# Second half of both value stages: nine couples of weight pieces as 2x2 block products, seven products for eight

## What is computed

```python
def peer_ffn(h, wq, keys, u, v):
    ...
    gates = jax.nn.softmax(sc, axis=-1)
    ...
        act = jax.nn.gelu(jnp.einsum('td,ted->te', ht, u[et]), approximate=False)
        return jnp.einsum('te,ted->td', gt * act, v[et])
```

## Time and profile before

| | |
|---|---|
| runs | 2201.31 us median (2198.94, 2201.31, 2205.94) |
| span of the profiled execution | 2200.3 us |
| PE busy | 2187.5 us, 99% |
| DVE busy | 1649.6 us, 75% |
| ACT busy | 1223.3 us, 56% |
| granted PE clock | full in all slices |

### The profile page before, as it was taken

How to read it: one execution, slowest core, us unless ns; L and a number is a source line. 1 busy time by engine, 2 the same in 40 slices (tenths; PEclk the granted TensorE clock), 3 DMA queues, 4 the chain that set the end, 5 groups by cost and what they waited for, 6 DMA issues and landing times.

```text
span 2200.3 us, 43642 instructions
## 1 busy us (share of the span) xinstructions
PE 2187.5 (99%) x14230; PEld 1905.3 (87%) x14230; DVE 1649.6 (75%) x3276; ACT 1223.3 (56%) x1933; POOL 719.4 (33%) x737
## 2 busy tenths in 40 slices
PE   9999999999999999999999999999999999999999
PEld 8899888888888888888988888888888888899887
DVE  8776885888888755666678678888886556558895
ACT  6555555555544445565565555554444446566764
POOL 1506886333344100002088853324440001530000
PEclk9999999999999999999999999999999999999999
DMA  5265665555655566554556655555556665545665
GB/s 175 97 200 156 189 188 176 172 172 170 187 177 179 180 193 191 172 192 134 173 172 186 188 180 173 172 167 187 174 179 193 203 194 172 163 141 159 187 190 162
DMA packets 109819, 385.88 MB, mean 175 GB/s; under 512 B 12545, under 2 KB 15009, under 8 KB 109473
## 3 DMA queue, kind: packets, MB, share of 16 engines
q1 hardware_dynamic: 106864, 382.34, 55.8%
q10 hardware_dynamic: 2864, 2.36, 0.3%
HBM read 383.46 MB, written 1.06 MB: 175 GB/s over the span
## 4 chain that ended last, share of the span: by engine, by line
PE 92%; DVE 5%; POOL 1%; DMA 1%; ACT 1%; issue 1%; SPq 0%; ACTq 0%; DVEq 0%; POOLq 0%
PE bank L2395 24%; PE bank L2367 13%; PE bank L2447 11%; PE bank L2449 11%; PE bank L2448 11%; PE bank L2283 3%; PE bank L2271 3%; PE bank L2275 3%; PE bank L2807 3%; PE bank L2590 1%; DVE w_lo L1259 1%; POOL big L506 1%; PE bank L2491 1%; PE bank L2492 1%; PE bank L2493 1%; PE bank L2775 1%
## 5 line engine op out<-in xcount | busy, mean ns | idle before, releaser
L583 ACT ACTIVATE w_hi<-ring 128x1024 fp32r<-128x1024 f32 x699 | 738.1, 1057 | 509.5 <-PE bank L2449 362.9
L1259 DVE TENSOR_TENSOR w_lo<-ring,w_hi 128x1024 fp32r<-128x1024 f32 x548 | 670.3, 1225 | 261.7 <-ACT w_hi L583 261.7
L2395 PE MATMUL bank<-x_parts,w_hi 128*128 128x512 f32 x2320 | 583.1, 393 | 0.3 <-ACT w_hi L583 0.3
L2395 PEld LDWEIGHTS bank<-x_parts,w_hi 128*128 128x128 f32 x2320 | 416.9, 189 | 75.0 <-issue 0.4
L467 POOL TENSOR_TENSOR w_lo<-ring,w_hi 128x1024 fp32r<-128x1024 f32 x151 | 364.2, 2418 | 266.0 <-DVE x_parts L1244 160.4
L2447 PE MATMUL bank<-w_hi,x_parts 128*128 128x512 f32 x1024 | 400.8, 391 | 0.0
L2449 PE MATMUL bank<-w_lo,x_parts 128*128 128x512 f32 x1024 | 398.7, 389 | 0.0
L2448 PE MATMUL bank<-w_hi,x_parts 128*128 128x512 f32 x1024 | 398.3, 389 | 0.0
L479 POOL COPY quads<-sco 128x32 f16 (+1 forms) x256 | 226.2, 912 | 445.7 <-DVE sco L1751 445.6
L2367 PEld LDWEIGHTS bank<-x_parts,w_lo 128*128 128x128 f32 x2368 | 324.3, 190 | 25.0 <-DVE w_lo L1259 2.9
L2367 PE MATMUL bank<-x_parts,w_lo 128*128 128x256 f32 x2368 | 335.7, 283 | 0.2 <-DVE w_lo L1259 0.2
(11 more groups left out here) (368 smaller groups left out, 2747.9 us busy)
## 6 DMA issues: line engine op xcount, KB each, us to landing
ring<-u_dram SPq DMA_DIRECT2D x256, 512.0 KB, 3.6
ring<-v_dram SPq DMA_DIRECT2D x256, 512.0 KB, 4.1
ring<-up_dram SPq DMA_DIRECT2D x44, 512.0 KB, 4.2
ring<-wq_dram SPq DMA_DIRECT2D x32, 512.0 KB, 4.2
ring<-sb_in_dram SPq DMA_DIRECT2D x31, 512.0 KB, 3.9
ring<-od_in_dram SPq DMA_DIRECT2D x25, 512.0 KB, 4.0
ring<-down_dram SPq DMA_DIRECT2D x22, 512.0 KB, 4.3
ring<-ev_in_dram SPq DMA_DIRECT2D x21, 512.0 KB, 3.7
```

The source lines that it names most:

```text
L583: A(w_hi[:, k % RING, :], ring[:, k % RING, :], ACT.Copy).then_inc(g["w_hi_done"], 1)
L1259: V.tensor_tensor(w_lo[:, k % RING, :], ring[:, k % RING, :], w_hi[:, k % RING, :].bitcast(F32), ALU.subtract).then_inc(g["lo_dve"], 1)
L2395: mm(dst[:, :], hi[:, rows[c]], x_both[:, c, :], start=(c == 0), stop=False, skip_group_check=True)
```

## The change

In the second half of each value stage 18 of the 64 pieces are taken as nine couples. A couple of pieces (two slices of experts) with two blocks of tokens and two of columns is a 2x2 block product by another 2x2. The change computes it with seven block products instead of eight, by Winograd's form of Strassen's scheme: it needs four sums of activation blocks and four of weight blocks for each couple. The results go to seven banks: the three that belong to one output block alone go straight to `bank[4]` to `bank[6]`, the other four are gathered over all couples in `bank[0]` to `bank[3]`, and are combined and added once at the end.

The other 46 pieces (`DIRECT`) are done as before: five ahead of the first couple, four between two couples, five more behind the last four. All of it is written out piece by piece; the loops of six are gone in the second half.

For each couple, DVE forms the sums (`pair_sums`, seven instructions) three pieces ahead, and the low parts of raw blocks, weight sums, activations and activation sums (`pair_part`, four instructions) in the three steps behind it. ACT rounds the same four groups one step earlier. SP loads the two raw pieces of a couple to a place of their own in `big` (two such places): the first two couples' in the middle of the first half, each later one as soon as DVE has done with its place.

At the end ACT copies `bank[0]` out, DVE forms the four combinations (four instructions) and adds them to `bank[4]` to `bank[7]` (four more) while PE does the last two pieces. The three tables of the last block (1 MB) are all loaded behind the last value piece of layer 1, ahead of the first piece of `sb_in`. Some semaphores are shared under new names, which changes no wait.

```diff
+HEAD, COUPLED, BETWEEN, TAIL = 5, 9, 4, 5
+DIRECT = HEAD + COUPLED * BETWEEN + TAIL
+CB = 512
...
+            def first_pairs(layer):
+
+                sp.wait_ge(g["pieces_used"], starts[f"v{layer}"] + 16)
+                load_pair(layer, 0)
+                load_pair(layer, 1)
...
+                for d in range(DIRECT):
+                    s = pair_after(d - 2)
+                    if 0 <= s < COUPLED - 2:
+                        sp.wait_ge(*pair_summed(layer, s, 6))
+                        sp.wait_ge(*pair_low(layer, 4 * s + 1))
+                        load_pair(layer, s + 2)
+                    sp.wait_ge(*low_bits(k0 + d - RING))
+                    load(a[f"v{layer}"][direct_row(d)], k0 + d)
...
+                for d in range(DIRECT):
+                    direct_chunk(d)
+                    for ahead, parts in ((3, (0,)), (2, (1,)), (1, (2, 3))):
+                        s = pair_after(d + ahead)
+                        if s >= 0:
+                            for part in parts:
+                                pair_part(s, part)
...
+                    V.tensor_tensor(b3(out[:, 0:2 * CB], 2), b12, b3(raw[:, CB:3 * CB], 2), ALU.subtract).then_inc(g["pair_summed"], 1)
+                    V.tensor_tensor(s1, a21, a22, ALU.add).then_inc(g["pair_summed"], 1)
+                    dve.wait_ge(*pair_summed(layer, s, 1))
+                    V.tensor_tensor(out[:, 2 * CB:3 * CB], raw[:, CB:2 * CB], out[:, CB:2 * CB], ALU.subtract).then_inc(g["pair_summed"], 1)
+                    dve.wait_ge(*pair_summed(layer, s, 2))
+                    V.tensor_tensor(a21, a21, a11, ALU.subtract).then_inc(g["pair_summed"], 1)
+                    V.tensor_tensor(s2, s1, a11, ALU.subtract).then_inc(g["pair_summed"], 1)
+                    dve.wait_ge(*pair_summed(layer, s, 3))
+                    V.tensor_tensor(out[:, 3 * CB:4 * CB], raw[:, 0:CB], out[:, 2 * CB:3 * CB], ALU.subtract).then_inc(g["pair_summed"], 1)
+                    dve.wait_ge(*pair_summed(layer, s, 5))
+                    V.tensor_tensor(s4, a12, s2, ALU.subtract).then_inc(g["pair_summed"], 1)
...
+                    for m, (x, w, to) in enumerate(((A12, B21, 4), (S4, B22, 5), (A11, B11, 0), (S3, T3, 3), (S1, T1, 1), (S2, T2, 2), (A22, T4, 6))):
+                        dst = bank[to][:, :]
+                        mm(dst, x_high[x], w_high[w], start=(s == 0 and to < 4), stop=False, skip_group_check=True)
+                        mm(dst, x_low[x], w_high[w], start=False, stop=False, skip_group_check=True)
+                        last = mm(dst, x_high[x], w_low[w], start=False, stop=False, skip_group_check=True)
...
+                for j in range(4):
+                    if j < 3:
+                        dve.wait_ge(*pair_free(layer, COUPLED, j + 1))
+                    else:
+                        dve.wait_ge(g["pieces_used"], k0 + DIRECT - 1)
+                    V.tensor_tensor(bank[4 + j][:, :], bank[4 + j][:, :], pair_ends[:, j * CB:(j + 1) * CB], ALU.add).then_inc(g["pair_low"], 1)
```

More of the change, by code:

```diff
@@ L82, in build @@
         bank = [ctx.enter_context(nc.psum_tensor(f"bank{i}", [P, 512], F32)) for i in range(8)]
+        with nc.sbuf_tensor("below_sums", [P, 8 * CB], F32), nc.sbuf_tensor("sums_low", [P, 8 * CB], F32R) as sums_low, \
+                nc.sbuf_tensor("parts", [P, 16 * CB], F32R) as parts:
+            pass
+        with nc.sbuf_tensor("below_acts", [P, 64 * T], F32), nc.sbuf_tensor("acts_low", [P, 64 * T], F32R) as acts_low:
+            pass
         big = sb("big", [P, 128 * T])
@@ L925, in experts @@
                 v_chunk(2)
[L926 to L939, removed]
+                loops = (HALF - RING) // BODY
+                with act.Fori(0, loops) as i:
+                    for j in range(BODY):
+                        high(first_v + RING + j, i)
+                        v_chunk(RING + j, i)
+                nh[0] += BODY * loops
+                for k in range(RING + BODY * loops, HALF):
+                    highs(first_v + k + 1)
+                    v_chunk(k)
+                act.wait_ge(g["gated"], 64 * layer + 64)
+                for d in range(DIRECT):
[5 more added lines that the diff above has]
+                                pair_part(s, part)
+                    if d == DIRECT - 3:
+                        act.wait_ge(*pair_free(layer, COUPLED - 1))
+                        A(pair_ends[:, 0:CB], bank[0][:, :], ACT.Copy).then_inc(g["pair_high"], 1)
+                n[0] += HALF + DIRECT
                 highs(n[0] + 2)
@@ new lines, in pair_part @@
+                def pair_part(s, part):
+                    b = s % 2
+                    row = couple_row(s)
+                    acts, low_acts = big[:, row * T:(row + 2) * T], acts_low[:, (row - HALF) * T:(row + 2 - HALF) * T]
+                    dve.wait_ge(*pair_high(layer, 4 * s + part + 1))
+                    dst, src, high = ((pair_lo[b], pair_raw[b][:, 0:3 * CB], pair_hi[b][0]), (pair_sum_low[s % 3], pair_sum[s % 3], pair_hi[b][1]),
+                                      (low_acts, acts, act_hi[b][:, 0:4 * P]), (act_sum_low[b], act_sum[b], act_hi[b][:, 4 * P:7 * P]))[part]
+                    V.tensor_tensor(dst, src, high.bitcast(F32), ALU.subtract).then_inc(g["pair_low"], 1)
@@ new lines, in experts @@
+                e11, e12, e21, e22 = (pair_ends[:, j * CB:(j + 1) * CB] for j in range(4))
+                for d in range(DIRECT):
+                    direct(d)
+                    if pair_after(d + 3) >= 0:
+                        pair_sums(pair_after(d + 3))
+                    for ahead, parts in ((2, (0,)), (1, (1,)), (0, (2, 3))):
+                        s = pair_after(d + ahead)
+                        if s >= 0:
+                            for part in parts:
+                                pair_part(s, part)
+                    if d == DIRECT - 3:
+                        dve.wait_ge(*pair_high(layer, 4 * COUPLED + 1))
+                        step(V.tensor_tensor(e21, bank[2][:, :], e11, ALU.add))
+                        settle()
+                        step(V.tensor_tensor(e12, bank[1][:, :], e21, ALU.add))
+                    if d == DIRECT - 2:
+                        settle()
+                        step(V.tensor_tensor(e22, bank[3][:, :], e12, ALU.add))
+                        step(V.tensor_tensor(e21, bank[3][:, :], e21, ALU.add))
```

193 lines of the change are left out of this document (153 added, 40 removed).

## The result

The changed kernel takes 2190.21 us, the median of four runs (2187.8 to 2193.5), beside 2202.16 us for the kernel before in the same comparison. The ratio is 0.9946, 95% interval 0.9932 to 0.9961. A second comparison of the same two kernels gave 2189.14 us and a ratio of 0.994 (0.9926 to 0.9954). The forecast was 2190.7 us.

The account below looks back on a forecast made before the run. PE's own pace was taken to bound the second value half. Span 2200.3, less 12.2 for 54 matmuls, plus 1.6 for late first couples, gives 2189.7; with 1.0 to the median, 2190.7 us, range 2187.0 to 2197.5.

Parts of the forecast that it names:

- What bounds the kernel, and what goes: Second half of the value stages: PE's own pace sets the end; 54 matmuls fewer at 0.2267 us save 12.2 us.
- DVE's load: Second value half: DVE needs 14.2 us per couple against PE's 15.6, going from 58% to 91% busy.
- Couples 2 to 9 cost nothing: Steady state of the second value half: PE's time in a couple and DVE's idle time cover the added work; charge 0.
- A charge at each couple: Rival at the start of couples: small waits of 0.3 us at each of 18, time 2196.1 us; chance 0.21.
- The first couple: Start of each second value half: piece 4 is late and PE loses 0.8 us once per layer, 1.6 in all.
- The lower bound in the prediction: At each layer's first couple: a loss of 0 if the sums cost only 3.0 us.
- Loads: Burst in SP's queue, first half: piece 33 about 1.3 us late at ACT; charge 0, at most 1.5 us per layer.
- The end: Four adds into PSUM at the end of the value stage: charge 0, upper bound 0.5 us per layer.
- DVE as the bound: Rival in the second value half: DVE's period passes PE's; at 17 us per couple the time is 2215; chance 0.07.
- The sum: Whole kernel: 2200.3 - 12.2 + 1.6 = 2189.7 us of span, median 2190.7, 0.5% less.

## Why the prediction was right, step by step

**What bounds the kernel, and what goes.** Shown. 54 matmuls by themselves gave 12.4 us for the 12.2 of the sum. The row's 0.2267 us holds within the couples too, with their other buffers and seven activation blocks. The page "TensorE: Matmul & The Clock Gate" of the Trainium skill, section "Back-to-back issue gap", gives about 131 ns for such a matmul, an estimate of 7.1 us for the 54; the run with only the matmuls left out decides for the row.

**DVE's load.** 14.2 us were laid out, 14.0 measured. The short sums were the uncertain rows, between 292 and 528 ns; they took 283, so the value near the lower bound was the right one. The 528 was no second price: it is the mean of eight, of which seven took 291 to 294 ns and one 2171, with POOL at work. The waits between dependent sums cost nothing that can be seen where another sum lies between:

```profile
L1986 DVE TENSOR_TENSOR parts<-big,parts 128x1536 fp32r<-128x1536 f32 x9 | 15.7, 1750 | 0.0
...
L1967 DVE TENSOR_TENSOR x_plain<-big 128x128 f32<-128x128 f32 x9 | 2.5, 283 | 0.0
```

The 1750 ns are the 1.76 of the straight line through the earlier trace rows. With one more sum, where nothing lies between the two, the first takes 1.25 us in starts (777.76 to 779.01 in that trace) for the 1.13 that it takes here (751.81 to 752.94), so a bare wait costs 0.1 us. DVE was laid out at 91% of a period and is at 90% in the stretch from 812 to 843 us.

**Couples 2 to 9 cost nothing.** Shown by the stretch from 765 to 922 us, and by the kernel with one more sum, in which even DVE at 99.8% holds PE up nowhere behind the first couple. "A charge at each couple" (the small waits, 2196.1) didn't occur: PE's starts stay 0.227 us apart into the couple and out of it. The margin was smaller than laid out, though: the last plain piece ahead of a couple is ready 1.9 us before PE wants it at the second couple and 2.5 us at the later ones, for "some 3 us".

**The first couple.** 0.8 us per layer, at piece 4: 0.85 measured, at piece 4. DVE's starts, shifted by the 3.1 us, follow the layout within 0.1 us: the sums at 751.81 (laid out 751.8), the low part of piece 2 at 754.96 (755.0), that of piece 3 at 758.10 (758.1), piece 4 ready at 763.3 (763.4). In the half as a whole it is 1.0 us per layer instead of 0.8: the first matmul behind the wait is followed after 0.31 us and not 0.23 (763.46, 763.77), and piece 4 then takes 2.84 us for 2.72. (PE's weight load shows 0.17 us of issue too, ahead of piece 3, where PE's starts show nothing of it.) The kernel with the first couple earlier, 0.05 us from the one with only the matmuls left out, shows that nothing else was in it. The lower bound in the prediction doesn't follow from its layout: sums of 3.0 us for 3.2 would have left 0.6 of the 0.8 us, not 0.

**Loads.** The burst made piece 33 of the first half late at ACT, and with it at DVE, but not at PE. ACT in the trace of after; the last row is of the second half:

```profile
649.57 1.06 ACT L666 ACTIVATE w_hi<-ring 128x1024 fp32r<-128x1024 f32 x1 [1.35 <-PE bank L2631]
654.99 1.06 ACT L666 ACTIVATE w_hi<-ring 128x1024 fp32r<-128x1024 f32 x1 [4.05 <-DMA ring<-v_dram]
...
765.00 1.06 ACT L666 ACTIVATE w_hi<-ring 128x1024 fp32r<-128x1024 f32 x1 [2.08 <-DMA ring<-v_dram]
```

Piece 33 comes 1.2 us after its old place (650.74 in the earlier trace rows, and 3.1 for the shift, is 653.83); 1.3 was laid out. DVE has the piece ready at 657.6, PE wants it at 659.0 (655.95 and 3.1). PE shows no wait in the half of the burst. That was a margin of 1.4 us, and of 1.1 at piece 34, not a comfortable one. The prediction had no late load in the second half; there was one per layer, at piece 6 (2.08 us at ACT in layer 0, 1.78 in layer 1). Its load was issued at 759.34, just behind a raw pair. DVE took the piece at 768.93 without having waited for it, so it cost nothing.

**The end.** 0 charged, 0 found: PE turns back at 920.83 and DVE's adds start at 921.53, 0.70 later; before, 922.86 and 923.55, 0.69 later. DVE stands idle for 0.42 us ahead of them, for 0.4 laid out.

**DVE as the bound.** It didn't occur, and its point was put right: the prediction had the gain eaten at 16.3 us of DVE per couple and a loss over 0.3% from 16.7. The kernel with two more sums has 16.5 and is 6 us slower than before. It lies a little nearer because a fuller DVE is also later at the first couple, by 2.5 us per layer, which that working left out.

**The sum.** By the halves, 2 x (174.25 - 169.14) = 10.2 us less, for 10.6 forecast; the 0.4 is the first couple, 1.0 us for 0.8 in either layer (a half of 169.1 us for the 168.8 laid out; the prediction also took 174.1 for the 174.25 of before). The measured 12.0 and 13.6 us between medians is somewhat more. The rest isn't the change's doing on PE: the kernel with 64 plain pieces is itself 1.75 us below the kernel before, by clock and by time around the span, and without that the changed kernel gains 10.2 by the first comparison and 11.9 by the second. Why the second gives more isn't shown. That the predicted median is right to 0.5 us is thus partly luck: the profiled span of before was 1.6 us above the median span of 21 other runs (2200.3 and 2198.7), and the time around the span, taken as 1.0 us, was 1.75 for the new kernel. The one made the forecast too high, the other too low, and with the 0.4 us of gain that was missing they nearly cancel.

## What to carry to other kernels

Where the matrix engine sets the pace, price removed matmuls by their start-to-start time and price the helper engine by its sum per period; then lay out the first period by itself, since the first one has no slack behind it, and prepare it a step earlier if it is late. An engine can stand at 100% and hold up nobody, or at 80% and hold up all: what decides is whether a wait for buffers stands ahead of work that the other engine needs in order to free them. Count the pieces between such a wait and the work behind it before more of the good thing is added.

## What the runs showed of the hardware that I had not expected

**The clock can fall behind a pause of about 2 us, or not.** In the kernel with thirteen couples PE's first pause of this kind in layer 0 lasts 3.86 us and eleven more 2.27 us each. Behind the second the matmuls start 0.56 and then 0.43 us apart for 3.1 us in all, then 0.227 again (stretches as above, granted clock third from the end):

```profile
776.47 0.76 PE L2672 MATMUL bank<-w_hi,x_parts 128*128 128x512 f32 x1 [2.27 <-DVE x_parts L1381]
777.03 0.63 PE L2673 MATMUL bank<-w_hi,x_parts 128*128 128x512 f32 x1
777.46 0.63 PE L2674 MATMUL bank<-w_lo,x_parts 128*128 128x512 f32 x1
```

```profile
776.40:779.50 3.10, 3.03 (x7) 2.48 (x8) 3.10 (x4) 2.44 (x5) 0.00 (x0) 0.50 0.51 174
```

That is the lower of the two levels, 1.2 GHz for 2.4. The same pause of 2.27 us at 790.66 was followed by matmuls 0.23 us apart, and that at 803.42 by a granted clock of 0.51 again. In either layer the pause of 3.86 us and six of the eleven of 2.27 were followed by the lower level. From one pause to the next it is 12.8 us where the clock stayed (790.66 to 803.42) and 14.2 to 14.4 where it fell (776.47 to 790.66, 803.42 to 817.77): a fall costs about 1.5 us. Seven of them are some 10 of the 31 us by which this half is longer than that of the kernel with the sums later; the rest is waiting.

Shorter pauses aren't safe either. With two more sums, the pause of 1.88 us ahead of the first couple left the granted clock at 1.00 in layer 0. In layer 1 the same pause was followed by the lower level (PE in layer 1, kernel with two more sums, and its stretch):

```profile
1680.71 0.47 PE L2676 MATMUL bank<-w_hi,x_parts 128*128 128x512 f32 x1 [1.88 <-DVE x_parts L1381]
...
1682.23 0.63 PE L2678 MATMUL bank<-w_lo,x_parts 128*128 128x512 f32 x1
1682.66 0.63 PE L2676 MATMUL bank<-w_hi,x_parts 128*128 128x512 f32 x1
```

```profile
1681.00:1686.00 5.00, 5.00 (x16) 3.94 (x15) 5.00 (x5) 3.95 (x7) 0.00 (x0) 0.66 0.86 281
```

It cost nothing in the end: that half is as long as the one in layer 0 (178.5 and 178.4 us), since DVE set the pace and PE's wait at the next couple was the shorter for it, 0.35 us for 0.57. The pauses of 0.6 to 0.7 us with one more and two more sums, and those of 0.6 and 2.0 us in the kernel with thirteen couples and later sums, were followed by no fall in either layer.

**The first 160 us differ between executions** of one and the same kernel by their granted clock, and this moves the whole (span 2186.0 at a mean clock of 1.000, 2191.8 at 0.997, both the changed kernel). Of its two traces one is 4.5 us longer than the other, and its half begins 4.7 us later. That is half of what this change brings; reading the half by itself is what makes a change of this size legible from one trace.
